# The roots of the mean squares taken as a power on GpSimd instead of a ScalarE root and a VectorE reciprocal

## What is computed

```python
def rms_norm(x, g):
    xf = x.astype(jnp.float32)
    y = xf * lax.rsqrt(jnp.mean(xf * xf, axis=-1, keepdims=True) + EPS)
    return (y * g.astype(jnp.float32)).astype(x.dtype)
...
    hp = hp + rms_norm(mp, g[1])
    hp = hp + rms_norm(swiglu(rms_norm(hp, g[2]), ffn_w_in[layer], ffn_w_out[layer]), g[3])
```

## Time and profile before

| | before |
|---|---|
| median of 3 runs | 1130.98 us (1130.73 to 1131.18) |
| span of the profiled execution | 1128.3 us; the time outside the span is 2.7 us against the median |
| PE busy | 1063.5 us (94%) |
| DVE busy | 508.4 us (45%) |
| ACT busy | 362.9 us (32%) |
| POOL busy | 103.2 us (9%) |
| granted clock of TensorE, mean | 0.968 |

### The profile page before, as it was taken

The page is one execution under the profiler, slowest core; times in us unless marked ns, Lnnn a source line. Parts: engine busy times, 40 slices in busy tenths (PEclk is TensorE's granted clock), DMA queues, the critical chain, the costliest instruction groups (busy, mean ns, idle before and its releaser), DMA issues.

```text
span 1128.3 us, 19561 instructions
## 1 busy us (share of the span) xinstructions
PE 1063.5 (94%) x8027; PEld 1035.0 (92%) x8027; DVE 508.4 (45%) x747; ACT 362.9 (32%) x598; POOL 103.2 (9%) x114
## 2 busy tenths in 40 slices
PE   6989989889999999999999788899999999999996
PEld 4788889879999999999999778799999999999995
DVE  4385743754444444432222659544444444322225
ACT  5421343443222222222222665322222222222222
POOL 0070220430000000000000325200000000000002
PEclk9998999899999999999999988899999999999998
DMA  6322112213332332323223210123223323232212
GB/s 216 94 62 78 39 38 76 58 38 95 96 88 75 95 90 75 91 74 91 87 78 101 64 42 20 54 79 97 87 76 94 90 76 92 72 91 88 88 52 80
DMA packets 166531, 89.67 MB, mean 79 GB/s; under 512 B 11976, under 2 KB 163647, under 8 KB 166492
## 3 DMA queue, kind: packets, MB, share of 16 engines
q1 hardware_dynamic: 164620, 86.99, 26.2%
q10 hardware_dynamic: 1648, 1.78, 0.5%
q0 software_dynamic: 224, 0.35, 0.1%
HBM read 86.53 MB, written 2.58 MB: 79 GB/s over the span
## 4 chain that ended last, share of the span: by engine, by line
PE 85%; DVE 9%; ACT 3%; issue 2%; DMA 1%; POOL 0%; SPq 0%; ACTq 0%; POOLq 0%; DVEq 0%
PE ps L452 27%; PE ps L454 27%; PE ps L453 27%; DVE h L1552 2%; DVE tmp L1535 2%; DVE wlo L1297 1%; PE ps L848 1%; PE ps L513 1%; DVE xlo L1539 1%; DMA x_tok<-in_x_sample_dram 1%; ACT whi L923 0%; DVE va L1356 0%; PE ps L497 0%; PE ps L661 0%; DVE acc_post L1523 0%
## 5 line engine op out<-in xcount | busy, mean ns | idle before, releaser
L452 PE MATMUL ps<-xhi,whi 128*128 128x272 f32 x1600 | 476.0, 297 | 26.8 <-DVE xlo L1539 15.3
L454 PE MATMUL ps<-xhi,wlo 128*128 128x272 f32 x1600 | 471.1, 294 | 0.0
L453 PE MATMUL ps<-xlo,whi 128*128 128x272 f32 x1600 | 469.0, 293 | 0.0
L452 PEld LDWEIGHTS ps<-xhi,whi 128*128 128x128 f32 x1600 | 309.7, 194 | 31.7 <-DVE xlo L1539 17.7
L1297 DVE TENSOR_TENSOR wlo<-raw,whi 128x1024 fp32r<-128x1024 f32 (+2 forms) x175 | 196.4, 1122 | 277.0 <-ACT whi L923 272.8
L453 PEld LDWEIGHTS ps<-xlo,whi 128*128 128x128 f32 x1600 | 310.4, 194 | 0.0
L454 PEld LDWEIGHTS ps<-xhi,wlo 128*128 128x128 f32 x1600 | 309.4, 193 | 0.0
L923 ACT ACTIVATE whi<-raw 128x1024 fp32r<-128x1024 f32 (+2 forms) x176 | 167.9, 954 | 205.4 <-PE ps L454 192.6
L452 PE MATMUL ps<-mhi,whi 128*128 128x272 f32 x704 | 204.2, 290 | 3.7 <-DVE tmp L1600 3.7
L454 PE MATMUL ps<-mhi,wlo 128*128 128x272 f32 x704 | 203.8, 290 | 0.0
L453 PE MATMUL ps<-mlo,whi 128*128 128x272 f32 x704 | 203.1, 288 | 0.0
(11 more groups left out here) (194 smaller groups left out, 850.2 us busy)
## 6 DMA issues: line engine op xcount, KB each, us to landing
raw<-in_ffn_w_in_dram SPq DMA_DIRECT2D x88, 512.0 KB, 3.8
raw<-in_ffn_w_out_dram SPq DMA_DIRECT2D x32, 384.0 KB, 3.1
raw<-in_ffn_w_out_dram SPq DMA_DIRECT2D x32, 320.0 KB, 2.9
raw<-in_ab_w_in_dram SPq DMA_DIRECT2D x10, 512.0 KB, 3.8
x_tok<-in_x_prompt_dram SPq DMA_DIRECT2D x4, 512.0 KB, 5.2
raw<-in_ab_w_in_dram SPq DMA_DIRECT2D x8, 256.0 KB, 3.5
raw<-in_ab_w_out_dram SPq DMA_DIRECT2D x8, 256.0 KB, 2.7
raw<-in_ab_w_out_dram SPq DMA_DIRECT2D x16, 128.0 KB, 3.2
```

The source lines that it names most:

```text
L452: pe.matmul(out, wh, xh, start=first, stop=False)
L453: pe.matmul(out, wh, xl, start=False, stop=False)
L454: return pe.matmul(out, wl, xh, start=False, stop=last)
```

## The change

The root on ACT and the reciprocal on DVE go. DVE instead adds eps to the mean squares (reading them from PSUM) and writes `ms`; POOL raises `ms` to the power -0.5 with a two-input operation against a tile `power` that holds -0.5. The factor 1/1024 moves into the column of ones and into the scale of the input's squares. The warm-ups for the root, and the wait that kept DVE from overwriting `rstd` ahead of `pool_out`, go. The cut diff:

```diff
-            def root_half(n, b):
-                act.wait_ge(sum_ready, n)
-                act.activation(rms[:, c], flat(6, 3 * b, 3), ACT.Sqrt, scale=1.0 / D, bias=eps[:, :]).then_inc(rms_ready, 1)
...
-            act.wait_ge(va_bn, NT)
-            act.activation(ln_rms[:, :], mean_var[:, :, 1], ACT.Sqrt, bias=eps[:, :]).then_inc(ln_rms_ready, 1)
             hi_part(7)
...
-                warm(ACT.Sqrt)
                 step(8)
-                root_half(1, 0)
                 step(9)
...
-                residual_half(0, 0, split, {0: lambda: step(10), 2: lambda: evacuate_out(11), 4: lambda: root_half(2, 1)})
+                residual_half(0, 0, split, {0: lambda: step(10), 2: lambda: evacuate_out(11)})
...
-            residual_half(1, 0, None, {0: last_and_diagonals, 3: lambda: root_half(5, 1),
-                                       5: lambda: keep_spread_half(5, 1)}, keep_turned_h)
+            residual_half(1, 0, None, {0: last_and_diagonals, 5: lambda: keep_spread_half(5, 1)}, keep_turned_h)
...
+            def guard(dst, mean):
+                return dve.tensor_scalar(dst, mean, EPS, None, ALU.add)
+
             def invert_half(n, b):
-                dve.wait_ge(rms_ready, n + 1)
-                if n == 7:
-
-                    dve.wait_ge(pool_out_ready, 1)
-                c = slice(3 * b, 3 * b + 3)
-                dve.reciprocal(rstd[:, c], rms[:, c]).then_inc(rstd_ready, 1)
+                dve.wait_ge(sum_ready, n)
+                guard(ms[:, 3 * b:3 * b + 3], flat(6, 3 * b, 3)).then_inc(ms_ready, 1)
...
-            dve.wait_ge(ln_rms_ready, 1)
-            dve.reciprocal(ln_rstd[:, :], ln_rms[:, :]).then_inc(ln_rstd_ready, 1)
+            dve.wait_ge(va_bn, NT)
+            dve.tensor_scalar(ln_ms[:, :], mean_var[:, :, 1], EPS, None, ALU.add).then_inc(ln_ms_ready, 1)
             dve.wait_ge(ln_rstd_ready, 1)
...
+            def invert(n, c0, c1, p=P):
+
+                pool.wait_ge(ms_ready, n + 1)
+                return pool.tensor_tensor(rstd[0:p, c0:c1], ms[0:p, c0:c1], power[0:p, c0:c1], ALU.pow)
+
+            invert(0, 0, NT).then_inc(rstd_ready, 1)
+            pool.wait_ge(ln_ms_ready, 1)
+            pool.tensor_tensor(ln_rstd[:, :], ln_ms[:, :], power[:, 0:NT], ALU.pow).then_inc(ln_rstd_ready, 1)
             pool.wait_ge(ln_loaded, 32)
...
+                invert(NORM_POST[s], 0, 3).then_inc(rstd_ready, 1)
                 for b in range(2):
...
                     for k in range(KC):
                         if s < 3:
                             add_square(s, b, k)
+                        if b == 0 and k == 4:
+                            invert(NORM_POST[s] + 1, 3, 6).then_inc(rstd_ready, 1)
                         if s in SHARED and k in (1, 3):
                             scale(b, k + 4)
...
             residual_halves(0, z)
             zero_sum(2)
+            invert(3, 0, NT).then_inc(rstd_ready, 1)
             residual_halves(1, z)
             zero_sum(5)
+            invert(6, NT - 1, NT, TAIL)
+            invert(6, 0, NT - 1).then_inc(rstd_ready, 1)
...
             residual_halves(2, z_pool)
             zero_sum(8)
+            invert(9, 0, NT).then_inc(rstd_ready, 1)
             residual_halves(3, z)
```

More of the change, by code:

```diff
@@ L213, in build @@
         ssq = sb("ssq", [P, NT])
-        rms = sb("rms", [P, 6])
+        ms = sb("ms", [P, 6])
         rstd = sb("rstd", [P, 6])
+        power = sb("power", [P, 6])
         eps = sb("eps", [P, 1])
@@ L260, in build @@
             mean_var = ab_sb("mean_var", [P, NT, 2])
-            ln_rms = ab_sb("ln_rms", [P, NT])
+            ln_ms = ab_sb("ln_ms", [P, NT])
             ln_rstd = ab_sb("ln_rstd", [P, NT])
@@ L297, in build @@
         ws_turned, wm_ready, kc_turned, kc_ready = sem("ws_turned"), sem("wm_ready"), sem("kc_turned"), sem("kc_ready")
-        sum_ready, rms_ready, rstd_ready = sem("sum_ready"), sem("rms_ready"), sem("rstd_ready")
+        sum_ready, ms_ready, rstd_ready, ln_ms_ready = sem("sum_ready"), sem("ms_ready"), sem("rstd_ready"), sem("ln_ms_ready")
         rstd_spread, r_ready = sem("rstd_spread"), sem("r_ready")
@@ L306, in build @@
         x_hi, x_lo = sem("x_hi"), sem("x_lo")
-        va_gelu, va_stats, va_bn, ln_rms_ready = sem("va_gelu"), sem("va_stats"), sem("va_bn"), sem("ln_rms_ready")
+        va_gelu, va_stats, va_bn = sem("va_gelu"), sem("va_stats"), sem("va_bn")
         ln_rstd_ready, va_normed, va_scaled, va_ready = sem("ln_rstd_ready"), sem("va_normed"), sem("va_scaled"), sem("va_ready")
@@ L932, in keep_spread_half @@
                 act.activation(r_post[:, frames(b)], flat(6, P, HALF), ACT.Copy).then_inc(r_ready, 1)
[L934 to L949, removed]
             def keep_spread(n, dst):
@@ L991, in _ @@
                     act.wait_ge(x_squared, t)
-                act.activation(u_raw[0:n, 0:2, 0:512], x_tok[0:n, t, :].rearrange("p (a b) -> p a b", a=2), ACT.Square,
+                act.activation(u_raw[0:n, 0:2, 0:512], x_tok[0:n, t, :].rearrange("p (a b) -> p a b", a=2), ACT.Square, scale=D ** -0.5,
                                accum_out=ssq[0:n, t:t + 1]).then_inc(x_squared, 1)
@@ L995, in _ @@
                     hi_part(2 + t // 3)
-            root(0)
             hi_part(4)
@@ L1138, in ffn_layer @@
             def ffn_layer(layer, n_post):
-                root(n_post + 1)
                 keep_spread(n_post + 1, r_pre)
@@ L1198, in _ @@
             evacuate_last(1, 0)
-            warm(ACT.Sqrt)
             hi_part(U_C)
-            root_half(4, 0)
             hi_part(U_C + 1)
@@ L1210, in last_and_diagonals @@
                 op.then_inc(diag_ready, 1)
-            residual_half(1, 0, None, {0: last_and_diagonals, 3: lambda: root_half(5, 1),
-                                       5: lambda: keep_spread_half(5, 1)}, keep_turned_h)
+            residual_half(1, 0, None, {0: last_and_diagonals, 5: lambda: keep_spread_half(5, 1)}, keep_turned_h)
             residual_half(1, 1, None, {}, keep_turned_h)
-            root(6)
             act.wait_ge(band_loaded, 64)
@@ L1249, in _ @@
                 pool_evacuate(e, 1)
-                if e == 3:
-                    root_half(7, 0)
                 if e == 4:
@@ L1256, in _ @@
             split_1 = lambda k: gain(1, 2, k)
-            residual_half(2, 0, split_1, {4: lambda: root_half(8, 1)})
+            residual_half(2, 0, split_1, {})
             keep_spread_half(8, 1)
@@ L1261, in _ @@
             evacuate_last(3, 0)
-            warm(ACT.Sqrt)
-            root_half(10, 0)
             keep_spread_half(10, 0)
             evacuate_last(3, 1)
-            root_half(11, 1)
             def keep_y(t, upper):
@@ L1298, in lo_part @@
                     .then_inc(w_lo, 1)
+            def guard(dst, mean):
+                return dve.tensor_scalar(dst, mean, EPS, None, ALU.add)
             def invert(n):
-                dve.wait_ge(rms_ready, n + 1)
+                if n == 0:
+                    dve.wait_ge(x_squared, NT)
+                    guard(ms[:, 0:NT], ssq[:, :]).then_inc(ms_ready, 1)
+                    return
+                dve.wait_ge(sum_ready, n)
                 if n == 6:
-                    dve.reciprocal(rstd[0:TAIL, NT - 1:NT], rms[0:TAIL, NT - 1:NT])
-                    dve.reciprocal(rstd[:, 0:NT - 1], rms[:, 0:NT - 1]).then_inc(rstd_ready, 1)
+                    guard(ms[0:TAIL, NT - 1:NT], flat(6, NT - 1, 1, TAIL))
+                    guard(ms[:, 0:NT - 1], flat(6, 0, NT - 1)).then_inc(ms_ready, 1)
                     return
-                dve.reciprocal(rstd[:, 0:NT], rms[:, 0:NT]).then_inc(rstd_ready, 1)
+                guard(ms[:, 0:NT], flat(6, 0, NT)).then_inc(ms_ready, 1)
             def invert_half(n, b):
-                dve.wait_ge(rms_ready, n + 1)
-                if n == 7:
-                    dve.wait_ge(pool_out_ready, 1)
-                c = slice(3 * b, 3 * b + 3)
-                dve.reciprocal(rstd[:, c], rms[:, c]).then_inc(rstd_ready, 1)
+                dve.wait_ge(sum_ready, n)
+                guard(ms[:, 3 * b:3 * b + 3], flat(6, 3 * b, 3)).then_inc(ms_ready, 1)
             dve.memset(wm_t[CHUNK:P, :, 0:CHUNK], 0.0)
@@ L1682, in _ @@
             pool.memset(ssq[:, :], 1.0)
-            pool.memset(ones[:, :], 1.0).then_inc(set_up, 1)
+            pool.memset(power[:, :], -0.5)
+            pool.memset(ones[:, :], 1.0 / D).then_inc(set_up, 1)
             pool.memset(k_s[:, DEC:CHUNK], 0.0)
```

## The result

The changed kernel takes 1136.49 us (median of 4 runs, 1135.4 to 1137.18) against 1130.86 beside it: ratio 1.0065, 95% interval 1.0045 to 1.0085. It is slower by 5.6 us between the medians, by 7.4 by the ratio; forecast were 1126.8 us and faster. The span went from 1128.3 to 1133.6 us. The time outside the span is 1.7 to 1.9 us in every run that lists both. The 2.7 us that the sum carried over came from setting one execution's span against the median of others.

The account below looks back on a forecast made before the run. PE was taken to bound the kernel (85% of the chain), so the change acts only where PE waits. The terms sum to -9.4 + 7X, -4.15 us at X = 0.75, giving 1126.8 us against 1130.98; range 1122.5 to 1134.

Parts of the forecast that it names:

- The layer norm: Normalisation starts earlier, PE's wait before its fourth projection shrinks: -4.4 us, and -2.1 us without the clock's fall, together -6.5.
- X: Time of one power on POOL, for 1 to 5 columns alike, taken as 0.75 us.
- my own formula: The summed effect of all places, -9.4 + 7X, with seven exposed powers; even at X = 1.34.
- n = 3 and 9: RMS norms ahead of the feed-forwards: PE's wait between sum and spread grows X - 0.25 each, +1.0 us for both.
- n = 5: At this RMS norm DVE's stall for ACT's root goes and half 1 starts earlier: -(3.1 - X), or -2.3 us.
- n = 6: At this RMS norm two additions and two powers in a row lose 2X - 0.5: +1.0 us.
- n = 7: At this RMS norm the power queues on POOL behind a weight unit's low part: +2.1 + X = +2.9 us.
- n = 11: At this RMS norm the power stands behind POOL's scaling: X - 0.5, +0.3 us.
- n = 2: At this RMS norm DVE's 0.65 us wait for ACT goes, of which 0.4 gets through: -0.4 us.
- n = 1, 4, 8, 10: RMS norms costed at nothing: slack or a POOL gap covers the power, at n = 1 up to X = 1.3.
- The slower side: Rival that the power is slow: over 0.2% slower from X = 1.67, 1140.6 us at 2.43; chance 0.16.
- The clock rival: Layer norm's stall goes but the clock's fall stays or comes elsewhere, at n = 7 for one: 1129 us; chance 0.08.

Follow-up runs that it names:

- experiment 1: Kernel before with only the layer norm's root taken as a power on GpSimd, the twelve RMS norms unchanged: 1121.9 us, ratio 0.9949.
- experiment 5: Kernel before with ScalarE's layer-norm root moved ahead of its two copies of the value projection, no power: 1121.91 us, ratio 0.9951.
- Experiment 4: Changed kernel with three unread products between sum and spread ahead of each feed-forward: 1131.34 us, ratio 1.0034.
- experiments 2 and 9: 2: changed kernel with the layer norm's root and reciprocal back on ScalarE and VectorE, 1142.61 us; 9: changed kernel again, unchanged, 1135.73 us.
- Experiment 7: Changed kernel with the powers of n = 5, 7 and 11 moved up POOL's queue: 1130.24 us, ratio 1.0022.
- experiment 6: Changed kernel with only the power of n = 7 moved ahead of the weight unit's low part on POOL's queue: 1134.09 us, ratio 1.0061.

## Why the prediction was wrong

**The layer norm: mechanism right, size off by the clock.** Start of the normalisation (55.45 forecast, 55.94 measured with X = 1.17), `v_t` at 64.4 and PE's wait under 1 us came as worked out. The trace gained 11.15 us (9.7 in the second trace of the kernel after), not 6.5, since the falls at the scores, where `L452` took 0.57 us at 104.91 in the trace of before, went too. In the time it is 5.8 to 6.8 us (experiment 1), near the forecast. The trace of before was one of its slower executions, and I made the sum against it without knowing how far its clock falls vary, so part of that agreement is luck. The step's cause was also put too narrowly: moving the root in ACT's queue gives the same (experiment 5).

**X: mis-sized.** I took 0.75 us, as "nearest to a whole small instruction". It was 0.85 to 1.07 for 3 columns, 1.17 for 5, 0.56 for one. The seven exposed powers cost 7.1 us, not 5.25: 1.8 us. By my own formula that gives a gain of 2.3 us still, so this term alone doesn't turn the sign.

**The first failing step was to price a PE wait at its length.** "X - 0.25 each" for n = 3 and 9 was exact as a wait: 1.51 - 0.58 = 0.93 at X = 1.18. But at n = 3 the clock fell with it. The spread took 0.74 us more and the head of the first feed-forward ran at 1.2 GHz: +2.67 us in a stage that I had left at zero. Experiment 4 gives 1.9 of that back by unread products alone. The Trainium skill (TensorE: Matmul & The Clock Gate, Why this matters for your kernels) warns of idle gaps between bursts of matmuls; the trace agrees in kind, with 1.00 falling to 0.50 at the end of the wait of 3.14 us at n = 5. I had used such a fall only on the side of the gain. The fall is not fixed to the wait, though. With the same wait at n = 3 there is none at the spread in experiments 2 and 9 (1.30 us). At n = 9 the clock is down in the trace of before as well, behind 0.58 us. So the +1.6 us of the second feed-forward are not shown to come from the wait at n = 9. They go with the fall in its middle, which experiment 1, with the old RMS norms, has too; its cause is open.

**n = 5: the sign was wrong, because a start gained was taken for an end gained.** "The power now stands on POOL behind the fifth square's addition": it did, at 631.49, which is about 638.4 less the 7.0 us by which this stage came earlier. DVE did finish half 0 near 633. But PE, with nothing to do for 3.14 us, fell to half clock, its spread took 1.38 for 0.84, and `r_post` was copied 1.4 us later than worked out. Half 1 began 0.65 us early instead of 2.3, and then took 11.5 us to the sum of n = 6 instead of 9.3: +1.55 instead of -2.3. Experiment 7, with the power three places up, separates the two. There half 1 begins 3.3 us earlier behind the sum of n = 4 than in before, and the stage (28.17 us) ends only 0.8 us earlier. DVE's pass over half 1 lasts 10.2 us for 7.7, more of its operations taking 0.99 us for 0.43 to 0.49 beside POOL's additions. So the place of the power cost 2.4 us here, and most of the gain that I had counted was not to be had.

**n = 7: right in kind, too small.** Forecast +2.9 at the start of the residual. In the trace the residual starts at 686.63, 13.19 us behind the sum, against 8.36 before: +4.8. X accounts for 0.3 and the longer spread for 0.6; the products behind it ran at 0.50 too, from 680.5 us on. From the sum of n = 7 to `r_pre` of n = 9 the loss is 6.4 us for 3.4, and experiment 6 takes all of it back in its trace (43.03 us; 45.54 in that of experiment 7).

**n = 11**: +0.3 forecast, +2.2 measured: 0.3 by X, 0.7 by the spread at half clock; the rest lies behind the spread, where the transposes run at 0.50 as well. **n = 6**: +1.0 forecast, +0.5 measured; **n = 2**: the 0.4 us forecast as a gain did not come (sum to copy 8.03 us, before 8.04). **n = 1, 4, 8, 10**: the covers held.

**The rivals.** The slower side came true, but not through the price and the point that I gave it (slow from X = 1.67): at X near 1.06 the kernel is slower already, as clock and queue take the place of a longer power. The clock rival existed only as a smaller gain; it should have been a loss where a new wait of PE appears.

## What to carry to other kernels

A wait added to TensorE costs its own length only if the clock stays up; where PE idles anew, price the work behind it at half clock as well, as an upper bound, and look whether PE has useful work to put there. Do not carry the gained start of a stage over to its end without asking what paces the stage. An operation moved to another engine takes the place of its listing in that engine's queue: put it where its input is ready (experiment 7 won some 5 to 6 us of time by moving three powers). Before moving work off an engine, try its place in that engine's own queue: here one move on ScalarE gave all of the gain and none of the loss.

## What was not expected of the hardware

- A power on GpSimd takes 0.56 us for 1 column, 0.85 for 3, 1.17 for 5: about 0.15 us a column and 0.4 fixed, against 0.2 for an addition. Close behind an operation of GpSimd on 272 or 1024 columns both take 0.2 us more (1.06 and 0.39 for 3 columns), which VectorE's work alone does not explain.
- Three products added ahead of each feed-forward made the changed kernel some 4 us faster (1131.34 for 1135.73 us).
- A wait of 1.51 us of PE at n = 3 brought the clock down at the spread in one trace of the changed kernel (2.04 us) and not in the other (1.30 us).
- The kernel before has times in two groups some 5 us apart, 1122 to 1126 and 1127 to 1131 us; one trace of it is not its median.
